# Ten of sixteen weight sums of a decoder block moved from ahead of and inside the recurrence to behind it

## The chip, the cores and the metric

One core of a Trainium2 chip runs the whole program. The metric is the device time of one execution in microseconds (us). The engines are named as in the profile: PE (TensorE), DVE (VectorE), ACT (ScalarE), POOL (GpSimd) and SP (SyncE, which here only issues transfers).

## The reference

One layer of a decoder trunk in fp32, over 2048 tokens of width 1024: a gated linear attention mixer, a 4-head attention into 256 memory tokens beside it, an output projection, and a squared-ReLU MLP of width 4096.

```
h = rms_norm(x, norm_mix)
y_mix, xq = gla_branch(h, ...)              # projections, then a chunked recurrence
y_mem = memory_cross_attention(xq, rms_norm(mem, norm_mem), w_kv)
x = x + concatenate([y_mix, y_mem]) @ w_out
x = x + sq_relu_mlp(rms_norm(x, norm_mlp), w_up, w_down)
return rms_norm(x, final_norm)
```

## The kernel before, in words

The 2048 rows are worked through in 4 blocks of 512. Block 0 is written out by itself, blocks 1 to 3 run in a loop. A block reads all weights again, in "chunks" of 1 MB: SP loads a chunk into one of two halves of `raw`, ACT rounds it to `w_hi` (`split_hi`), DVE takes the rest `w_lo = raw - w_hi` (`split_lo`), and PE makes three products of each pair of operands. Chunk `i` is loaded when the parts of chunk `i - 2` have been made, and split when PE is done with chunk `i - 2`.

A block has these stages, by chunk number: queries of the memory attention (0, 1), then q, k (2 to 5; with the gate's running sum, on DVE, line 1290, and the memory attention), v and the output gate r (6 to 13), the output projection (`C_OUT` = 14 to 19), and the MLP (from `C_MLP` = 20; its chunks are counted by `s` from 0). In stage 6 to 13 the recurrence runs beside the projections: 16 half steps `hs`, each a ring of POOL (products with decays, `rung_products`), PE (`L1694`), DVE (gaps) and ACT (exponentials).

The MLP's order is 5 "up" chunks, 7 "down" chunks, 4 up, 7 down, 4 up, 7 down, 3 up, 7 down. The down product is made by a scheme with 7 products instead of 8 on sums of quarters of the activations (DVE, `u_parts`) and of the weights. The weights' sums don't depend on the block. So they are made once, in block 0, in 16 steps of 1 MB, and kept in DRAM in `w_mix`. Of each seven down chunks four are read from `w_mix` and three from `w_down`. One step `j` is: SP loads two rows of quarters of `w_down` into a slot (`mix_load`), POOL makes four subtractions of 128x512 in place (`mix_sums`, lines 652 to 659), and SP stores the slot (`mix_store`). A slot is a piece of on-chip memory that something else uses at other times. In the kernel before there are three: a piece over `y_rows` and the inner state, the upper half of `sr`, and `u_parts`. The first two are in use during the recurrence's later half, and `u_parts` in the MLP.

SP works through its own list in order. Where the transfers of the sums stand in it is a table by chunk number, written by hand (`mix_work`). A load of a slot waits until the slot's last store has landed. A store waits for POOL's sums. Everything behind them on SP, the chunk loads too, waits with them. The kernel before does steps 0 to 11 on POOL ahead of the recurrence's first product, and steps 12 to 15 behind half steps 1, 3, 7 and 9 of the recurrence in block 0.

`xres` holds the block's residual rows; it is loaded at `C_OUT + 3`. `xin` holds the next block's x; it is loaded at MLP position `s` = 4, squared by ACT and scaled by DVE later in the MLP, and transposed by PE in the last seven down chunks. Block 0's own x was in `xin` and is last read at some 50 us.

Of the kernel before, what the change touches and what calls it, by code (L numbers as in the profile page):

```python
# [96 lines left out]
C_OUT = C_R + 4  # L97
# [12 lines left out]
UPS = HIDDEN // FCOLS  # L110
GROUPS = 4
DEPTH = UPS // GROUPS
RING = DEPTH + 1
HALF = BLOCK // 2
OPERANDS = 7
# [15 lines left out]
PIECES = 2  # L131

MIX_STEPS = UPS
MIX_EARLY = 12
MIX_LATE = {1: 12, 3: 13, 7: 14, 9: 15}

STEPS = 2 * (C_OUT - C_V)

# [135 lines left out]
def build(nc, x, mem, norm_mix, norm_mem, w_kv, w_out, norm_mlp, w_up, w_down, w_in, w_gate2, b_gate,  # L274
          out_gain, final_norm, rung_masks, identity, scan_mask, w_mix, out):
    with ExitStack() as ctx:
# [3 lines left out]
        def sem(name):  # L280
            return ctx.enter_context(nc.semaphore(name))
# [75 lines left out]


        mix_slots = [over_y_and_state[:], sr[:, 4:8, :], u_parts[:].rearrange("p (b x) t -> p b (x t)", b=4)]
        a_parts = u_parts[:, 0:4:3, :]  # L360
        b_parts = u_parts[:, 1:3, :]

# [65 lines left out]
        sums_ready = Signal(sem("sums_ready"), 0, UPS)  # L428
        u_hi_ready = Signal(sem("u_hi_ready"), 0, 2 * UPS)
        u_ready = Signal(sem("u_ready"), 2, 2 * UPS)  # L430
        mix_loaded = [sem(f"mix_loaded{s}") for s in range(3)]
        mix_made = sem("mix_made")
        mix_step = sem("mix_step")
        mix_stored = [sem(f"mix_stored{s}") for s in range(3)]
        out_ready = Signal(sem("out_ready"), 0, TILES)
        dve_step = sem("dve_step")

# [76 lines left out]
        def last_piece(i):  # L514

            return PIECES * i + PIECES - 1

        def mix_slot(j):

            return j % 3 if j < MIX_EARLY else 1 + j % 2  # L520

        def mix_uses(j):

# [2 lines left out]
        def mlp_source(s):  # L526

            if MLP[s][0] == "up":
                return wup[:, :, FCOLS * MLP[s][1]:FCOLS * (MLP[s][1] + 1)], KD
            g, operand = MLP[s][1], PRODUCTS[MLP[s][2]][2]  # L530
            if operand >= T1:
                return w_mix[:, g, operand - T1, :, :], DEPTH
            row, col = {B11: (0, 0), B21: (1, 0), B22: (1, 1)}[operand]
            return wdown[:, 2 * DEPTH * g + row:2 * DEPTH * (g + 1):2, 512 * col:512 * (col + 1)], DEPTH

# [19 lines left out]
        @block.sync  # L555
        def _(sp):
            def load(n, i, source, kblocks):

                sp.wait_ge(*hi_split.at(n, last_piece(i - 2)))
                sp.wait_ge(*lo_split.at(n, last_piece(i - 2)))  # L560
                sp.dma_start(as_kblocks(raw, i % 2, kblocks), source).then_inc(raw_loaded[i % 2].sem, 16)

            def mix_load(j):

                slot = mix_slot(j)
                if mix_uses(j):
                    sp.wait_ge(mix_stored[slot], 16 * mix_uses(j))
                to = mix_slots[slot].rearrange("p (k d) c -> p k (d c)", k=2)
                sp.dma_start(to, wdown[:, 2 * j:2 * j + 2, :]).then_inc(mix_loaded[slot], 16)

            def mix_store(j):

                slot = mix_slot(j)
                sp.wait_ge(mix_made, j + 1)
                sp.dma_start(w_mix[:, j // DEPTH, :, j % DEPTH, :], mix_slots[slot]).then_inc(mix_stored[slot], 16)

            mix_work = {1: [(mix_store, 0), (mix_load, 2)], 2: [(mix_store, 1), (mix_load, 3)],
                        3: [(mix_store, 2), (mix_load, 4), (mix_store, 3), (mix_load, 5)],
                        4: [(mix_store, 4), (mix_load, 6), (mix_store, 5), (mix_load, 7)],
                        5: [(mix_store, 6), (mix_load, 8), (mix_store, 7), (mix_load, 9)],  # L580
                        6: [(mix_store, 8), (mix_load, 10), (mix_store, 9), (mix_load, 11)],
                        7: [(mix_store, 10), (mix_store, 11)], 8: [(mix_load, 12), (mix_load, 13)],
                        10: [(mix_store, 12)], 11: [(mix_load, 14), (mix_store, 13)], 12: [(mix_load, 15)],
                        13: [(mix_store, 14)], 15: [(mix_store, 15)]}

            def load_block(n, x_row, x_next, first):
                for i in range(1, C_MLP):
                    load(n, i, chunk_source(i), KD if i < C_V or C_R <= i < C_OUT else KG)
                    if first:
                        for work, j in mix_work.get(i, ()):  # L590
                            work(j)
                    if i == C_OUT + 3:

                        sp.wait_ge(*read(n, ("oT", TILES - 1, 1)))
                        sp.dma_start(xres[:, :, :], x_tiles[:, bass.ds(x_row, TILES), :])\
                            .then_inc(xres_loaded.sem, 16)
                for s in range(len(MLP)):
                    if s == DEPTH:

                        sp.wait_ge(*weights_used.at(n, last_piece(C_MLP - 1)))  # L600
                        sp.dma_start(xin[:, :, :], x_tiles[:, bass.ds(x_next, TILES), :])\
                            .then_inc(xin_loaded.sem, 16)
                        for slot in range(3):
                            sp.wait_ge(mix_stored[slot], 16 * sum(mix_slot(j) == slot for j in range(MIX_STEPS)))
                    load(n, C_MLP + s, *mlp_source(s))
                load(n, CHUNKS, chunk_source(0), KD)

            sp.dma_start(xres[:, 0:MT, :], mem_tiles).then_inc(mem_loaded, 16)
            for i in range(KV_CHUNKS):
                if i >= 2:  # L610
                    sp.wait_ge(*hi_split.early(last_piece(i - 2)))
                    sp.wait_ge(*lo_split.early(last_piece(i - 2)))
                sp.dma_start(as_kblocks(raw, i % 2, KD), wkv[:, :, FCOLS * i:FCOLS * (i + 1)])\
                    .then_inc(raw_loaded[i % 2].sem, 16)
                if i == 1:
                    sp.dma_start(xin[:, :, :], x_tiles[:, 0:TILES, :]).then_inc(xin_loaded.sem, 16)
                    for tile, source in [(wg_raw, win[:, :, COL_G:COL_G + RANK]), (scan_raw, scan_mask),
                                         (masks_raw, rung_masks), (gain_o[:], out_gain), (gate_bias[:], b_gate),
                                         (gain_mlp[:], norm_mlp),
                                         (gain_fin[:], final_norm.rearrange("(a d) -> a d", a=1).broadcast_to([P, D]))]:  # L620
                        sp.dma_start(tile, source).then_inc(consts_loaded, 16)
            load(0, 0, chunk_source(0), KD)
            mix_load(0)
            mix_load(1)
            load_block(0, 0, TILES, True)
            with sp.Fori(1, BLOCKS) as n:
                load_block(n, sp.snap(n * TILES), sp.snap(((n + 1) % BLOCKS) * TILES), False)
# [3 lines left out]
        def _(pool):  # L631
# [29 lines left out]

            for j in range(MIX_EARLY):
                mix_sums(j)

            def rung_products(n, c, rung):


# [26 lines left out]
            def pool_block(n, first):  # L694
                for f in range(2):

                    pool.wait_ge(*read(n, ("k", 2 + f)))
                def o_rsqrt(c):
                    pool.wait_ge(*o_ms_ready.at(n, c))
                    nc.gpsimd.tensor_tensor(o_rstd[:, c, :], o_ms[:, c, :], minus_half[:], ALU.pow)\  # L700
                        .then_inc(o_rstd_ready.sem, 1)

                def y_low(c, p):
                    pool.wait_ge(*y_hi_ready.at(n, p * TILES + c))
                    hi = at_chunk(h_hi[:, 4 * p:4 * p + 4, :].bitcast(F32), c)
                    nc.gpsimd.tensor_tensor(at_chunk(h_lo[:, 4 * p:4 * p + 4, :], c), heads_of(y_row(c)), hi,  # L706
                                            ALU.subtract).then_inc(mix_ready.sem, 1)

                for hs in range(STEPS):
                    c = hs // 4  # L710
                    rung_products(n, c, hs % 4)
                    if hs % 4 == 0 and c:
                        end_products(n, c - 1)
                    if hs in (10, 12, 14):
                        o_rsqrt(hs // 2 - 5)
                    if first and hs in MIX_LATE:
                        mix_sums(MIX_LATE[hs])
                end_products(n, TILES - 1)
                o_rsqrt(TILES - 1)
                for p in range(2):  # L720
                    for c in range(TILES):
                        y_low(c, p)
                for which in range(3):
                    for t in range(TILES):
                        rsqrt(n, which, t)

            pool_block(0, True)
            with pool.Fori(1, BLOCKS) as n:
# [1271 lines left out]
```

## Time and profile before

| | |
|---|---|
| median of 3 runs | 2612.5 us (2611.78 to 2613.19) |
| the profiled execution | 2613.3 us, its span 2611.5 us |
| PE busy | 2540.9 us (97% of the span) |
| DVE, ACT, POOL busy | 59%, 46%, 17% |
| DMA | 339 MB, mean 130 GB/s |

The span runs from the first to the last instruction of the profiled execution; its own time is 1.8 us more. Idle time of an engine ahead of an instruction is shown with what ended it, as `[2.75 <-DVE u_lo L1456]`. `x2` behind a row says that it merges two instructions. SPq rows are transfers being issued; their landing is shown in another view.

### The profile page before, as it was taken

Reading aid. Unit: us, or ns where it says so; the run is one execution under the profiler, and the core shown is the slowest. Engines: PE = TensorE matmul, PEld = TensorE weight load, DVE = VectorE, ACT = ScalarE, POOL = GpSimd, SP = SyncE. Lnnn points to the kernel's source line nnn. Section 1 sums busy time; section 2 is a strip of 40 time slices with the busy share of each in tenths; the row PEclk is TensorE's granted clock in tenths of the full one; section 3 lists DMA queues with packets and bytes.
Section 4 is the critical chain, followed back from the end, with each engine's and each line's share of the span. In section 5 each row is a group of like instructions: output and inputs, shape, how many; then the busy total and the mean of one; then the engine's idle time right before and its main releaser. Section 6 shows DMA issues by size and latency. Waiting matters only on the chain.

```text
span 2611.5 us, 34630 instructions
## 1 busy us (share of the span) xinstructions
PE 2540.9 (97%) x11968; PEld 2125.4 (81%) x11968; DVE 1546.5 (59%) x2255; ACT 1205.5 (46%) x1752; POOL 445.6 (17%) x411
## 2 busy tenths in 40 slices
PE   6898999999999999999999999999999999999998
PEld 5687888888878888888878888888887888888886
DVE  5566646566746644666565663565665566465666
ACT  4433435444554434454445342545545444355444
POOL 4656400000003430000000541000000254000000
PEclk9999999999999999999999999999999999999999
DMA  8843234344422223443452213344433221343443
GB/s 295 295 164 122 65 115 167 122 161 146 165 95 65 65 100 127 148 136 122 144 178 65 81 50 119 123 149 158 145 131 129 81 65 53 124 163 124 150 155 135
DMA packets 191880, 339.41 MB, mean 130 GB/s; under 512 B 7025, under 2 KB 118769, under 8 KB 183505
## 3 DMA queue, kind: packets, MB, share of 16 engines
q1 hardware_dynamic: 188768, 328.36, 37.8%
q10 hardware_dynamic: 2928, 8.66, 0.8%
q8 instruction: 108, 1.77, 0.3%
q14 instruction: 76, 0.61, 0.1%
HBM read 311.84 MB, written 25.17 MB: 129 GB/s over the span
## 4 chain that ended last, share of the span: by engine, by line
issue 48%; PE 40%; POOL 5%; DVE 4%; ACT 1%; DMA 1%; DVEq 0%; ACTq 0%; POOLq 0%; SPq 0%
PE banks L1548 11%; PE banks L1550 11%; PE banks L1549 11%; PE banks L1694 3%; POOL queries L681 2%; PE banks L1674 1%; POOL h_lo L706 1%; POOL rstd L638 1%; PE banks L1735 1%; PE banks L1733 1%; PE banks L1718 1%; POOL keys L679 1%; DVE w_lo L1090 1%; DMA raw<-in_w_kv 1%; DVE sr L1288 1%
## 5 line engine op out<-in xcount | busy, mean ns | idle before, releaser
L1548 PE MATMUL banks<-h_hi,w_hi 128*128 128x512 f32 (+1 forms) x1760 | 678.1, 385 | 11.5 <-DVE h_lo L1109 4.7
L1550 PE MATMUL banks<-h_hi,w_lo 128*128 128x512 f32 (+1 forms) x1760 | 669.5, 380 | 0.0
L1549 PE MATMUL banks<-h_lo,w_hi 128*128 128x512 f32 (+1 forms) x1760 | 669.4, 380 | 0.0
L1090 DVE TENSOR_TENSOR w_lo<-raw,w_hi 128x2048 fp32r<-128x2048 f32 x144 | 344.9, 2395 | 296.5 <-ACT w_hi L738 296.5
L738 ACT ACTIVATE w_hi<-raw 128x2048 fp32r<-128x2048 f32 x144 | 275.5, 1913 | 271.2 <-PE banks L1548 241.8
L1548 PEld LDWEIGHTS banks<-h_hi,w_hi 128*128 128x128 f32 x1760 | 332.1, 189 | 77.5 <-issue 16.3
L1550 PEld LDWEIGHTS banks<-h_hi,w_lo 128*128 128x128 f32 x1760 | 331.8, 189 | 63.4
L1549 PEld LDWEIGHTS banks<-h_lo,w_hi 128*128 128x128 f32 x1760 | 332.1, 189 | 61.1
L1548 PE MATMUL banks<-w_hi,u_hi 128*128 128x512 f32 x896 | 351.8, 393 | 0.0
L1550 PE MATMUL banks<-w_hi,u_lo 128*128 128x512 f32 x896 | 349.1, 390 | 0.0
L1549 PE MATMUL banks<-w_lo,u_hi 128*128 128x512 f32 x896 | 348.8, 389 | 0.0
L745 ACT ACTIVATE w_hi<-raw 128x1024 fp32r<-128x1024 f32 x224 | 230.3, 1054 | 235.0 <-PE banks L1548 137.9
L1097 DVE TENSOR_TENSOR w_lo<-raw,w_hi 128x1024 fp32r<-128x1024 f32 x224 | 265.2, 1218 | 82.5 <-ACT w_hi L745 82.4
L638 POOL TENSOR_TENSOR rstd<-ms,minus_half 128x1 f32<-128x1 f32 x48 | 30.1, 631 | 1511.0 <-DVE ms L1101 1511.0
L1384 DVE TENSOR_TENSOR xres<-banks,xres 128x512 f32<-128x512 f32 x256 | 173.3, 688 | 120.0 <-PE banks L1550 119.3
L1548 PE MATMUL banks<-w_hi,h_hi 128*128 128x512 f32 (+1 forms) x544 | 215.0, 395 | 1.6 <-ACT v L813 1.2
L999 ACT ACTIVATE u_parts<-banks 128x512 f32<-128x512 f32 x128 | 76.2, 596 | 295.3 <-PE banks L1550 168.2
L1550 PE MATMUL banks<-w_hi,h_lo 128*128 128x512 f32 (+1 forms) x544 | 209.1, 384 | 0.0
L1549 PE MATMUL banks<-w_lo,h_hi 128*128 128x512 f32 (+1 forms) x544 | 209.1, 384 | 0.0
L1550 PEld LDWEIGHTS banks<-w_hi,u_lo 128*128 128x128 f32 x896 | 168.2, 188 | 35.4
L1549 PEld LDWEIGHTS banks<-w_lo,u_hi 128*128 128x128 f32 x896 | 168.3, 188 | 34.1
L1548 PEld LDWEIGHTS banks<-w_hi,u_hi 128*128 128x128 f32 x896 | 168.3, 188 | 33.9
(162 smaller groups left out, 3166.6 us busy)
## 6 DMA issues: line engine op xcount, KB each, us to landing
raw<-in_w_up SPq DMA_DIRECT2D x64, 1024.0 KB, 5.4
raw<-w_mix SPq DMA_DIRECT2D x64, 1024.0 KB, 4.7
raw<-in_gla_w_in SPq DMA_DIRECT2D x57, 1024.0 KB, 5.1
raw<-in_w_down SPq DMA_DIRECT2D x48, 1024.0 KB, 4.6
raw<-in_w_out SPq DMA_DIRECT2D x24, 1024.0 KB, 4.9
xin<-in_x SPq DMA_DIRECT2D x5, 2048.0 KB, 11.6
xres<-in_x SPq DMA_DIRECT2D x4, 2048.0 KB, 7.8
out<-xres ACTq DMA_DIRECT2D x16, 512.0 KB, 3.6
```

The lines of the kernel that those rows point to most:

```text
L638: nc.gpsimd.tensor_tensor(rstd[:, which, t:t + 1], ms[:, which, t:t + 1], minus_half[:, 0:1], ALU.pow).then_inc(rstd_ready.sem, 1)
L681: last = nc.gpsimd.tensor_tensor(kind_cols(queries, w, kind), spans(at_chunk(q, c), w, first, count), kind_cols(query_dec, w, kind), ALU.mult)
L738: nc.scalar.activation(w_hi[:, i % 2, :], raw[:, i % 2, :], ACT.Copy).then_inc(hi_split.sem, PIECES)
L745: nc.scalar.activation(w_hi[:, i % 2, at], raw[:, i % 2, at], ACT.Copy).then_inc(hi_split.sem, 1)
L999: nc.scalar.activation(part, banks[:, f, :].rearrange("p (h t) -> p h t", h=2), ACT.Relu)\
L1090: nc.vector.tensor_tensor(w_lo[:, i % 2, :], raw[:, i % 2, :], w_hi[:, i % 2, :].bitcast(F32), ALU.subtract).then_inc(lo_split.sem, PIECES)
L1097: nc.vector.tensor_tensor(w_lo[:, i % 2, at], raw[:, i % 2, at], w_hi[:, i % 2, at].bitcast(F32), ALU.subtract).then_inc(lo_split.sem, 1)
L1384: nc.vector.tensor_tensor(xres[:, t, cols], bank(name), xres[:, t, cols], ALU.add)\
L1548: after_chunk(pe.matmul(to, left[0], right[0], start=start, stop=False, skip_group_check=goes_on))
L1549: pe.matmul(to, left[0], right[1], start=False, stop=False, skip_group_check=goes_on)
L1550: return pe.matmul(to, left[1], right[0], start=False, stop=stop, skip_group_check=goes_on)
L1694: ins = pe.matmul(bank(name)[:, (h % 2) * COLS:(h % 2 + 1) * COLS], left, queries[:, h, :], start=True, stop=True)
```

## The change

Steps 0 to 5 stay ahead of the recurrence, in the same three slots. Steps 6 to 15 get two new slots, the two halves of `xin`. POOL makes sums 6 and 7 behind its last work for the mixer's output (`y_low`), and sums 8 to 15 behind the four `rsqrt` of the MLP's norm. SP loads slots for 6 and 7 behind the load of `xres` at chunk `C_OUT + 3`, and the other transfers stand in the MLP's first 14 chunks. The next x is now loaded at `s` = 15 in every block, once both new slots have been stored, which is ahead of up chunk 8 instead of up chunk 4.

```
-MIX_EARLY = 12
-MIX_LATE = {1: 12, 3: 13, 7: 14, 9: 15}
+NEXT_X = 15
+MIX_EARLY = 6
+MIX_IN_OUT = 8
...
+        mix_slots += [xin[:, 2 * s:2 * s + 2, :].rearrange("p t (b c) -> p (t b) c", b=2) for s in range(2)]
...
-            return j % 3 if j < MIX_EARLY else 1 + j % 2
+            return j % 3 if j < MIX_EARLY else 3 + j % 2
...
                 for s in range(len(MLP)):
-                    if s == DEPTH:
+                    if s == NEXT_X:
                         sp.wait_ge(*weights_used.at(n, last_piece(C_MLP - 1)))
+                        for slot in range(3, 5):
+                            sp.wait_ge(mix_stored[slot], 16 * sum(mix_slot(j) == slot for j in range(MIX_STEPS)))
                         sp.dma_start(xin[:, :, :], x_tiles[:, bass.ds(x_next, TILES), :])\
                             .then_inc(xin_loaded.sem, 16)
...
-                    if first and hs in MIX_LATE:
-                        mix_sums(MIX_LATE[hs])
                 end_products(n, TILES - 1)
                 o_rsqrt(TILES - 1)
                 for p in range(2):
                     for c in range(TILES):
                         y_low(c, p)
+                if first:
+                    for j in range(MIX_EARLY, MIX_IN_OUT):
+                        mix_sums(j)
                 for which in range(3):
                     for t in range(TILES):
                         rsqrt(n, which, t)
+                    if first and which == 0:
+                        for j in range(MIX_IN_OUT, MIX_STEPS):
+                            mix_sums(j)
```

In the loads of the MLP, SP also waits, ahead of each first down chunk, until the stores are done that its group reads.

POOL, in block 0, the first two products of the recurrence, in the kernel before: between the products of half step 1 (`keys`, `queries`) and those of half step 2 stand the four subtractions of step 12, in the slot in `sr`.

```order
L674 TENSOR_TENSOR queries<-q,near_dec 128x4x64
L679 TENSOR_TENSOR keys<-k,key_dec 128x512
L681 TENSOR_TENSOR queries<-q,query_dec 128x4x96
L681 TENSOR_TENSOR queries<-q,query_dec 128x4x64
L681 TENSOR_TENSOR queries<-q,query_dec 128x4x32
L652 TENSOR_TENSOR sr<-sr 128x512
L654 TENSOR_TENSOR sr<-sr 128x512
L656 TENSOR_TENSOR sr<-sr 128x512
L659 TENSOR_TENSOR sr<-sr 128x512
L679 TENSOR_TENSOR keys<-k,key_dec 128x512
L681 TENSOR_TENSOR queries<-q,query_dec 128x4x96
```

The same place in the changed kernel has the products alone; ahead of it stand 24 subtractions instead of 48.

POOL, in block 0, from the last of the mixer's output rows (`h_lo`) on, in the changed kernel: two sums of four subtractions in `xin`, the four `rstd` of the MLP's norm, and then the first of eight more sums. Before, the twelve `rstd` stood here by themselves.

```order
L721 TENSOR_TENSOR h_lo<-y_rows,h_hi 128x4x128 x2
L668 TENSOR_TENSOR xin<-xin 128x512
L670 TENSOR_TENSOR xin<-xin 128x512
L672 TENSOR_TENSOR xin<-xin 128x512
L675 TENSOR_TENSOR xin<-xin 128x512
L668 TENSOR_TENSOR xin<-xin 128x512
L670 TENSOR_TENSOR xin<-xin 128x512
L672 TENSOR_TENSOR xin<-xin 128x512
L675 TENSOR_TENSOR xin<-xin 128x512
L654 TENSOR_TENSOR rstd<-ms,minus_half 128x1 x4
L668 TENSOR_TENSOR xin<-xin 128x512
L670 TENSOR_TENSOR xin<-xin 128x512
```

SP, in block 0, from the load of `xres` to the second down chunk, in the kernel before: four up chunks, the next x, the fifth up chunk and the down chunks.

```order
L595 DMA xres<-in_x 128x4x1024
L561 DMA raw<-in_w_out 128x4x512 x2
L561 DMA raw<-in_w_up 128x8x256 x4
L601 DMA xin<-in_x 128x4x1024
L561 DMA raw<-in_w_up 128x8x256
L561 DMA raw<-in_w_down 128x4x512
```

The middle of the same stretch in the changed kernel, the third to the fifth up chunk and the first down chunk: each chunk load is now followed by a store of one step and the load of the step after the next, which goes into the same slot.

```order
L563 DMA raw<-in_w_up 128x8x256 x2
L577 DMA w_mix<-xin 128x4x512
L571 DMA xin<-in_w_down 128x2x1024
L563 DMA raw<-in_w_up 128x8x256
L577 DMA w_mix<-xin 128x4x512
L571 DMA xin<-in_w_down 128x2x1024
L563 DMA raw<-in_w_up 128x8x256
L577 DMA w_mix<-xin 128x4x512
L571 DMA xin<-in_w_down 128x2x1024
L563 DMA raw<-in_w_down 128x4x512
```

## Rows read from the trace of the kernel before

**Rows 1.** The page, its first part: busy time and share of the span.
```profile
PE 2540.9 (97%) x11968; PEld 2125.4 (81%) x11968; DVE 1546.5 (59%) x2255; ACT 1205.5 (46%) x1752; POOL 445.6 (17%) x411
```

**Rows 2.** ACT's timeline, block 0, q and k stage: start us, us, instruction.
```profile
91.50 0.66 ACT L806 ACTIVATE q<-banks 128x512 f32<-128x512 f32 x1
...
113.13 0.47 ACT L813 ACTIVATE v<-banks,neg_top 128x256 f32<-128x256 f32 x1 [11.52 <-DVE neg_top L1176]
...
123.44 1.94 ACT L738 ACTIVATE w_hi<-raw 128x2048 fp32r<-128x2048 f32 x1
```

**Rows 3.** ACT's timeline, block 1, the same three instructions.
```profile
746.87 0.65 ACT L806 ACTIVATE q<-banks 128x512 f32<-128x512 f32 x1
...
760.87 0.47 ACT L813 ACTIVATE v<-banks,neg_top 128x256 f32<-128x256 f32 x1 [3.90 <-DVE neg_top L1176]
...
769.01 1.94 ACT L738 ACTIVATE w_hi<-raw 128x2048 fp32r<-128x2048 f32 x1
```

**Rows 4.** SP's timeline: the load of xres in blocks 0 and 1.
```profile
326.81 0.37 SPq L595 DMA_DIRECT2D xres<-in_x  x1
...
957.12 0.39 SPq L595 DMA_DIRECT2D xres<-in_x  x1
```

**Rows 5.** DVE instructions by line: duration ns min/median/max, first and last start.
```profile
L1288 DVE SCALAR_TENSOR_TENSOR sr<-b,sr x16: 664/668/1715, 97.0 to 2018.2; 128x512 f32<-128x512 f32 x16
L1090 DVE TENSOR_TENSOR w_lo<-raw,w_hi x144: 2278/2293/3377, 57.6 to 2598.0; 128x2048 fp32r<-128x2048 f32 x144
L1174 DVE TENSOR_REDUCE top<-banks x32: 677/691/693, 112.1 to 2056.3; 128x2 f32<-128x512 f32 x32
```

**Rows 6.** POOL's timeline, block 0: parts of steps 11 and 12, then two rstd.
```profile
114.25 3.38 POOL L656 TENSOR_TENSOR over_y_and_state<-over_y_and_state 128x512 f32<-128x512 f32 x1
...
164.65 1.30 POOL L652 TENSOR_TENSOR sr<-sr 128x512 f32<-128x512 f32 x1
...
169.26 1.35 POOL L659 TENSOR_TENSOR sr<-sr 128x512 f32<-128x512 f32 x1
...
370.94 0.56 POOL L638 TENSOR_TENSOR rstd<-ms,minus_half 128x1 f32<-128x1 f32 x1 [40.41 <-DVE ms L1101]
...
378.40 0.55 POOL L638 TENSOR_TENSOR rstd<-ms,minus_half 128x1 f32<-128x1 f32 x1 [2.74 <-DVE ms L1101]
```

**Rows 7.** SP's timeline, block 0: the loads of chunk 4 and of MLP chunk 4.
```profile
77.65 0.37 SPq L561 DMA_DIRECT2D raw<-in_gla_w_in  x1
...
397.12 0.37 SPq L561 DMA_DIRECT2D raw<-in_w_up  x1
```

**Rows 8.** Transfers: issues, KB each, median us from issue to landing.
```profile
raw<-in_w_up SPq DMA_DIRECT2D x64, 1024.0 KB, 5.4
...
u_parts<-in_w_down SPq DMA_DIRECT2D x6, 1024.0 KB, 7.3
...
w_mix<-u_parts SPq DMA_DIRECT2D x6, 1024.0 KB, 8.7
```

**Rows 9.** PE's waits from 340 to 400 us: total, times, longest.
```profile
PE banks L1548 <- DVE h_lo L1399: 0.7, 1, 0.7
```

**Rows 10.** DVE's and ACT's timeline in block 0's MLP.
```profile
387.48 2.29 DVE L1090 TENSOR_TENSOR w_lo<-raw,w_hi 128x2048 fp32r<-128x2048 f32 x1 [0.83 <-ACT w_hi L738]
...
390.41 0.60 ACT L999 ACTIVATE u_parts<-banks 128x512 f32<-128x512 f32 x1 [3.03 <-PE banks L1550]
...
403.48 1.91 ACT L738 ACTIVATE w_hi<-raw 128x2048 fp32r<-128x2048 f32 x1
...
409.82 0.60 ACT L999 ACTIVATE u_parts<-banks 128x512 f32<-128x512 f32 x1 [2.75 <-DVE u_lo L1456]
...
413.19 0.60 ACT L999 ACTIVATE u_parts<-banks 128x512 f32<-128x512 f32 x1 [2.11 <-PE banks L1550]
...
414.36 1.91 ACT L738 ACTIVATE w_hi<-raw 128x2048 fp32r<-128x2048 f32 x1
...
450.53 2.03 ACT L745 ACTIVATE w_hi<-raw 128x1024 fp32r<-128x1024 f32 x2 [3.41 <-DMA raw<-w_mix]
```

More of the change, by code:

```diff
@@ L430, in build @@
         u_ready = Signal(sem("u_ready"), 2, 2 * UPS)
-        mix_loaded = [sem(f"mix_loaded{s}") for s in range(3)]
+        mix_loaded = [sem(f"mix_loaded{s}") for s in range(5)]
         mix_made = sem("mix_made")
         mix_step = sem("mix_step")
-        mix_stored = [sem(f"mix_stored{s}") for s in range(3)]
+        mix_stored = [sem(f"mix_stored{s}") for s in range(5)]
         out_ready = Signal(sem("out_ready"), 0, TILES)
@@ L575, in mix_store @@
                 sp.dma_start(w_mix[:, j // DEPTH, :, j % DEPTH, :], mix_slots[slot]).then_inc(mix_stored[slot], 16)
[L577 to L584, printed above, removed]
+            mix_work = {1: [(mix_load, 2)], 2: [(mix_store, 0), (mix_load, 3)], 3: [(mix_store, 1), (mix_load, 4)],
+                        4: [(mix_store, 2), (mix_load, 5)], 6: [(mix_store, 3)], 7: [(mix_store, 4)],
+                        8: [(mix_store, 5)], C_OUT + 3: [(mix_load, 6), (mix_load, 7)],
+                        C_OUT + 5: [(mix_store, 6), (mix_load, 8)], C_MLP: [(mix_store, 7), (mix_load, 9)],
+                        C_MLP + 2: [(mix_store, 8), (mix_load, 10)], C_MLP + 3: [(mix_store, 9), (mix_load, 11)],
+                        C_MLP + 4: [(mix_store, 10), (mix_load, 12)], C_MLP + 5: [(mix_store, 11), (mix_load, 13)],
+                        C_MLP + 6: [(mix_store, 12)], C_MLP + 7: [(mix_store, 13)], C_MLP + 8: [(mix_load, 14)],
+                        C_MLP + 9: [(mix_load, 15)], C_MLP + 12: [(mix_store, 14)], C_MLP + 13: [(mix_store, 15)]}
             def load_block(n, x_row, x_next, first):
@@ L588, in load_block @@
                     load(n, i, chunk_source(i), KD if i < C_V or C_R <= i < C_OUT else KG)
-                    if first:
-                        for work, j in mix_work.get(i, ()):
-                            work(j)
                     if i == C_OUT + 3:
@@ L596, in load_block @@
                             .then_inc(xres_loaded.sem, 16)
+                    if first:
+                        for work, j in mix_work.get(i, ()):
+                            work(j)
                 for s in range(len(MLP)):
-                    if s == DEPTH:
+                    if s == NEXT_X:
                         sp.wait_ge(*weights_used.at(n, last_piece(C_MLP - 1)))
+                        for slot in range(3, 5):
+                            sp.wait_ge(mix_stored[slot], 16 * sum(mix_slot(j) == slot for j in range(MIX_STEPS)))
                         sp.dma_start(xin[:, :, :], x_tiles[:, bass.ds(x_next, TILES), :])\
                             .then_inc(xin_loaded.sem, 16)
+                    if MLP[s] == ("down", 0, 0):
                         for slot in range(3):
                             sp.wait_ge(mix_stored[slot], 16 * sum(mix_slot(j) == slot for j in range(MIX_STEPS)))
+                    if s and MLP[s][0] == "down" and MLP[s - 1][0] == "up" and MLP[s][1] < GROUPS - 1:
+                        for slot in range(3, 5):
+                            made = sum(mix_slot(j) == slot for j in range(DEPTH * (MLP[s][1] + 1)))
+                            if made:
+                                sp.wait_ge(mix_stored[slot], 16 * made)
                     load(n, C_MLP + s, *mlp_source(s))
+                    if first:
+                        for work, j in mix_work.get(C_MLP + s, ()):
+                            work(j)
                 load(n, CHUNKS, chunk_source(0), KD)
@@ L722, in pool_block @@
                         y_low(c, p)
+                if first:
+                    for j in range(MIX_EARLY, MIX_IN_OUT):
+                        mix_sums(j)
                 for which in range(3):
```

## The prediction

> **What bounds the kernel now.** I read the page first: PE is busy 97% of the span [rows 1]. So only time in which PE is idle, or waits in a ring with other engines, can be won. The sums exist in block 0 alone, and block 1 does the same work without them. The next views are therefore the timelines of blocks 0 and 1, the same instruction in both, and the distance between them. Where the distance shrinks, block 0 has lost time that block 1 did not lose.
>
> - The copy of q starts at 91.50 in block 0 and at 746.87 in block 1: 655.37 apart. The split of the weights at the end of the first two score tiles starts at 123.44 and 769.01: 645.57 apart [rows 2, 3]. Block 0 loses 9.8 us between them. The reader sees where: ACT waits 11.52 us for DVE's `neg_top`, 3.90 us in block 1.
> - The load of xres is issued at 326.81 and 957.12: 630.31 apart [rows 4]. Block 0 loses another 645.57 - 630.31 = 15.3 us, all of it between 123 and 327 us, where the recurrence is.
>
> The first loss is DVE's. The gate's running sum is four pairs of an instruction `sr<-b,sr` and a scan. The first takes up to 1715 ns in block 0, against a median of 668 ns: 1.05 us more [rows 5]. If the scans are held as long, eight instructions make 8.4 us, and POOL is making sums 9 to 11 beside them. The second loss is POOL's own: step 12 takes from 164.65 to 170.61, 6.0 us [rows 6], in a ring whose next product stands behind it. Four such steps are 24 us of POOL, of which 15.3 us, or 3.8 us a step, reached the end.
>
> **What is removed.** Sums 6 to 11 leave the q and k stage and sums 12 to 15 leave the recurrence. If nothing else changed, block 0 would run both stretches as block 1 does: -9.8 - 15.3 = **-25.1 us**.
>
> **What remains ahead of the recurrence.** The six early steps are spread thinner. Step 5 is the last: its slot is stored behind the load of chunk 4, at some 78 us [rows 7]. A store lands in 8.7 us and a slot's load in 7.3 us [rows 8]: the load is issued at 87 and lands at 94 us. The sum then takes 5 to 6 us, until 99. DVE's chain begins at 97.0 [rows 5]. So at most two of its instructions are held by 1.05 us each: 0 to 2.1 us. I take +1.0, the middle, since which comes first depends on a microsecond.
>
> **What is added, the sums' time on POOL.** POOL is empty from 331 us on but for `rstd` (370.94 to 378.95, an idle stretch of 40.41 us before it) [rows 6]. Sums 6 and 7 fit in that stretch: their slots are loaded at 327 us behind the 2 MB of xres, land by 337 and 340, and the sums are done by some 349. Nothing there waits for POOL before 370.94. PE's waits from 340 to 400 us are 0.7 us in all [rows 9], so there is no idle time on PE to win, and each delay has to be judged by its slack.
>
> **Sums 8 and 9** run from 378.95 to some 391. DVE works there on the norm and then on the second MLP chunk's `w_lo`, 387.48 to 389.77. PE finishes the first chunk's bank at about 390.4 [rows 10]: 0.6 us of slack. One POOL instruction in the way costs such a `w_lo` up to 1.08 us (3377 - 2293 ns) [rows 5]: 0.5 us on PE. With a second hold in the norm it could be 2. I take +0.5, range 0 to 2.
>
> **Sums 10 to 13** fall into the up chunks, 10.88 us each (403.48 to 414.36) [rows 10]. What PE waits for next is the bank that ACT empties once DVE has written `u_lo`: ACT starts at 409.82 and is done at 410.42, PE is done with the other bank at about 413.2 [rows 10]. The slack is 2.8 us. A sum is four POOL instructions, so it holds DVE up by at most 4 x 1.05 = 4.2 us, and DVE idles in each chunk, so that nothing adds up. The high end is 1.4 us a sum, 5.6 us. But DVE is at work in about 6 of 11 us, so that two holds are likelier than four, and two fit. I take 0, range 0 to 5.6.
>
> **Sums 14 and 15** fall into the down chunks. There a chunk's split starts when its load lands (ACT's start at 450.53, after 3.41 us of waiting for the transfer) [rows 10], and two slot loads now go between those chunk loads. A load beside others lands in 7.3 instead of 5.4 us [rows 8], 1.9 us later, and DVE is held on top of it, 1.05 us. PE is gapless there too by what the page says of the whole, so some slack is there, but no row gives it. I take +0.5, range 0 to 3.
>
> **The transfers.** SP issues ten loads and ten stores in its list of chunk loads and is blocked while it waits for a store to land. From a store to the next store of the same slot it takes 8.7 (store) + 7.3 (load) + 6.0 (sum) = 22 us [rows 6, 8], and two up chunks are 21.8 us. That holds the pace, just. The chunk loads get 3 to 4 us later than the 397.12 of before [rows 7]. A chunk loaded then is split at 414.36 [rows 10], 17.2 us later, and needs 5.4 to 7.3 us to land [rows 8]. Less the 3 to 4 us that is some 7 us to spare, or 10 in all. I take 0. The next x moves by eleven chunks, but its first reader, ACT's square, stands behind the second down chunk of the next group, more than 20 us later at these paces, and 2 MB are two transfers of 5.4 us. Blocks 1 to 3 do nothing else new: 0.
>
> **The rule on the shared port.** The instruction `sr<-b,sr`, held by 1.05 us, has two inputs in on-chip memory, and the reduction from a PSUM bank, which ran at 112.1 us beside sum 11, never took over 693 ns [rows 5]. The Trainium skill, "SBUF — State Buffer", section "Who interferes with whom", states it as a rule: a VectorE instruction with two SBUF inputs and a GpSimd one that reads SBUF exclude each other, the one that comes later blocks until the first is done, and one with a PSUM input is free. By that rule the adds into xres in the down chunks are never held, and `w_lo`, `u_parts` and `u_lo` all can be. The trace agrees. The rule speaks against the change in one point: the lock works both ways, so that DVE's long `w_lo` stretches the sums, and by it the steps could fall behind the chunks. That is rival B.
>
> **The sum.** -25.1 + 1.0 + 0.5 + 0 + 0.5 = **-23.1 us**. The profiled execution took 2613.3 us, 0.8 us over the median, so I set it against both: 2613.3 - 23.1 = 2590.2, and from the median 2612.5 - 23.1 = **2589.4 us**.
>
> **Rivals.**
> - **A: DVE is held where it matters.** All the high ends at once are 2.1 + 2 + 5.6 + 3 = 12.7 us: 2612.5 - 25.1 + 12.7 = 2600. For it: sums 10 to 13 follow the landing of their loads, which follows DVE's `w_lo`, so the overlap may be the same in each chunk. Against it: the 2.8 us.
> - **B: SP's list falls behind.** A POOL instruction took 3.38 us beside `w_lo`, against 1.3 [rows 6]: 2.1 us more. Two of them in a sum and 2 us more for each transfer give 22 + 4.2 + 4 = 30 us for two chunks, 8.2 late, and three pairs 25 us. Less the 10 us to spare this puts PE 15 us behind: 2589.4 + 15 = 2604. It decides from 3 us late per pair on. Against it: the transfers would all have to be slow together.
> - **C, slower: a sum costs as much here as in the recurrence.** If each of the ten costs the 3.8 us that a late step cost, they cost 38 us, and the time is 2612.5 - 25.1 + 38 = **2625**. The place would be DVE's queue in the up and down chunks, and it decides from 2.5 us a sum. For it: PE is gapless here, so that any delay beyond the slack shows in full. Against it: in the recurrence the sum stood in POOL's own part of the ring, and here POOL has no part in one.
> - **D: nothing to be measured.** The 25 us come back as about as much loss, 2607 to 2618, by a mixture of A and B.
>
> **Chances.** Forecast (2586.5 to 2594) 0.62, A (2594 to 2600) 0.19, B and what lies between it and D (2600 to 2607) 0.08, C 0.07, D 0.04. The range reaches from 1 us under the full gain (2587.4) to the end of A: 2586.5 to 2600. A measurement of this kernel tells 0.2%, 5 us, from no change: faster 0.88, same 0.04, slower 0.08.
>
> **What would show it.** In the changed profile: ACT's wait for `neg_top` near 113 us falls from 11.5 to 4 to 6 us; xres is loaded 23 to 25 us earlier, at 302 to 304; at most one of the four `sr<-b,sr` of block 0 is over 1 us; POOL's sums stand between 313 and 440; PE's waits in the MLP of block 0 stay under 2 us; the distance from the load of xres to the first load of block 1's chunks is as before within 2 us. I would be wrong if PE's chunk pace in the first up chunks were over 10.9 us (A or C, with DVE as the releaser), or if ACT's splits there waited for transfers (B). The weakest steps are the zero for sums 10 to 13 and the zero for SP.

## The result, and the profile after

The changed kernel takes 2597.7 us in the median of 4 runs (2593.1 to 2598.5), against 2612.1 us for the kernel before: a ratio of 0.9939, 95% interval 0.9927 to 0.9952. The quotient of the two medians is 0.9945, inside that interval. The kernel is faster, by 14.4 us or 0.6%. That lies inside the range of 2586.5 to 2600, and 8.3 us above the 2589.4 of the forecast. The profiled execution took 2597.05 us, 16.25 less than the one before.

Two distances say where the time went. This is SP's timeline of the changed kernel, the load of `xres` in blocks 0 and 3, by the summary of its line (duration ns, first and last start us):

```profile
L595 SPq DMA_DIRECT2D xres<-in_x x4: 367/382/393, 302.6 to 2201.2; - x4
```

Before, block 0's stood at 326.8 [rows 4] and block 3's at 2217.4. So 24.3 us were won ahead of block 0's load of `xres`. From it to block 3's it was 1890.6 us, three times 630.2, and it is 1898.6 now: 8.0 us were lost behind it. 24.3 - 8.0 = 16.3 us is the difference of the two profiled executions.

Not all of what was won is waiting that went away. PE does the same work, 742 instructions, between 158 and 326.8 us as in block 1 between 803.6 and 957.1 us. These are the two stretches in the kernel before (length, PE's busy time and instructions; at the end the granted clock, the DMA share and GB/s):

```profile
803.60:957.10 153.50, 151.02 (x742) 129.27 (x742) 98.68 (x200) 67.69 (x129) 72.48 (x69) 1.00 0.20 62
158.00:326.80 168.80, 156.82 (x742) 132.99 (x741) 109.01 (x200) 67.29 (x128) 98.53 (x85) 0.97 0.29 94
```

Block 0's stretch is 15.3 us longer. For 5.8 us of that PE was busy, with the same instructions at a mean granted clock of 0.97 instead of 1.00, and for 9.5 us it waited. In slices of 10 us the clock is down, to 0.83 to 0.93, from 170 to 190, from 200 to 210 and from 250 to 260, each time where PE has just waited for over 2 us. In the changed kernel it is 1.00 in each slice from 70 to 330 us.

What answers to [rows 2] is ACT's timeline of the changed kernel in the q and k stage of block 0:

```profile
92.19 0.65 ACT L825 ACTIVATE q<-banks 128x512 f32<-128x512 f32 x1
...
106.45 0.47 ACT L832 ACTIVATE v<-banks,neg_top 128x256 f32<-128x256 f32 x1 [4.16 <-DVE neg_top L1195]
...
114.59 1.95 ACT L757 ACTIVATE w_hi<-raw 128x2048 fp32r<-128x2048 f32 x1
```

The wait is 4.16 us instead of 11.52, close to block 1's 3.90 [rows 3]. The stretch from the first to the last row is 22.4 us, where it was 31.9. DVE there, which answers to the first of [rows 5]:

```profile
97.65 0.95 DVE L1307 SCALAR_TENSOR_TENSOR sr<-b,sr 128x512 f32<-128x512 f32 x1 [4.57 <-ACT sr L896]
98.64 1.22 DVE L1309 TENSOR_TENSOR_SCAN b<-scanm,sr 128x512 f32<-128x512 uint8 x1
99.78 0.67 DVE L1307 SCALAR_TENSOR_TENSOR sr<-b,sr 128x512 f32<-128x512 f32 x1
```

One instruction is held up by POOL (I call that a hold), by the last sum, for 0.3 us, and no other.

The loss is in the MLP. PE's waits in block 0 of the changed kernel, to 660 us (total, times, longest), where [rows 9] had the single wait of 0.7 us from 340 to 400:

```profile
PE banks L1567 <- ACT u_parts L1018: 4.4, 3, 1.5
...
PE banks L1567 <- DVE w_lo L1109: 1.5, 1, 1.5
...
PE banks L1567 <- DVE h_lo L1418: 0.7, 1, 0.7
PE banks L1567 <- DVE w_lo L1116: 0.7, 1, 0.7
```

The three waits for ACT stand in the up chunks. PE's queue of weight loads shows more of each: idle for 5.9 us in four pieces between 366 and 425 us (before, 0.3 in one piece).

```profile
PEld banks L1567 <- issue: 5.9, 4, 1.9
```

Why ACT is late is in DVE's timeline of the changed kernel, one up chunk:

```profile
368.59 0.43 DVE L1461 TENSOR_TENSOR u_parts<-u_parts 128x256 f32<-128x256 f32 x1 [2.41 <-ACT u_parts L1021]
369.05 0.42 DVE L1462 TENSOR_TENSOR u_parts<-u_parts 128x256 f32<-128x256 f32 x1
369.40 1.52 DVE L1463 TENSOR_TENSOR u_parts<-u_parts 128x256 f32<-128x256 f32 x1
370.95 1.39 DVE L1464 TENSOR_TENSOR u_parts<-u_parts 128x256 f32<-128x256 f32 x1
372.27 3.39 DVE L1109 TENSOR_TENSOR w_lo<-raw,w_hi 128x2048 fp32r<-128x2048 f32 x1
375.58 3.18 DVE L1475 TENSOR_TENSOR u_lo<-u_parts,u_hi 128x768 fp32r<-128x768 f32 x2
...
381.24 0.43 DVE L1461 TENSOR_TENSOR u_parts<-u_parts 128x256 f32<-128x256 f32 x1 [2.48 <-ACT u_parts L1021]
```

POOL's timeline of the changed kernel over the same stretch, which is sum 10:

```profile
369.12 1.52 POOL L668 TENSOR_TENSOR xin<-xin 128x512 f32<-128x512 f32 x1 [1.79 <-DMA xin<-in_w_down]
370.59 1.47 POOL L670 TENSOR_TENSOR xin<-xin 128x512 f32<-128x512 f32 x1
372.02 1.49 POOL L672 TENSOR_TENSOR xin<-xin 128x512 f32<-128x512 f32 x1
373.59 3.22 POOL L675 TENSOR_TENSOR xin<-xin 128x512 f32<-128x512 f32 x1
```

Sum 10 starts 0.5 us after DVE's chain has begun. Sums 11, 12 and 13 start 0.8, 0.2 and 0.2 us after theirs. From there the two engines take turns: each of POOL's four subtractions holds one DVE instruction. In the kernel before, the same instructions took 0.42, 0.42, 2.29 [rows 10] and, for the pair, 2.09 us, as these two lines of DVE's timeline show:

```profile
404.41 0.42 DVE L1444 TENSOR_TENSOR u_parts<-u_parts 128x256 f32<-128x256 f32 x1
...
407.70 2.09 DVE L1456 TENSOR_TENSOR u_lo<-u_parts,u_hi 128x768 fp32r<-128x768 f32 x2
```

So the holds are 1.10 + 0.97 + 1.10 + 1.09 = 4.3 us. ACT's first instructions of the next chunks show what it does to the pace; they answer to [rows 10]:

```profile
378.79 0.60 ACT L1018 ACTIVATE u_parts<-banks 128x512 f32<-128x512 f32 x1 [5.35 <-DVE u_lo L1475]
...
391.47 0.60 ACT L1018 ACTIVATE u_parts<-banks 128x512 f32<-128x512 f32 x1 [5.34 <-DVE u_lo L1475]
...
403.99 0.60 ACT L1018 ACTIVATE u_parts<-banks 128x512 f32<-128x512 f32 x1 [4.25 <-DVE u_lo L1475]
...
416.58 0.60 ACT L1018 ACTIVATE u_parts<-banks 128x512 f32<-128x512 f32 x1 [4.32 <-DVE u_lo L1475]
```

An up chunk takes 12.7, 12.5 and 12.6 us instead of 10.9. The second down chunk's split, which PE's end with the last up chunk released at 435.18 before, stands at 417.75, 17.4 us earlier instead of 24.3, so ACT and DVE are 6.8 us behind there.

PE itself lost less. It does the same instructions in the same order in both kernels, so that equal counts mark the same point. Up to the end of the up chunks, first the kernel before and then the changed one:

```profile
0.00:427.97 427.97, 383.13 (x1911) 325.18 (x1912) 244.17 (x375) 181.55 (x306) 184.54 (x151) 0.97 0.51 176
0.00:408.92 408.92, 377.79 (x1911) 321.11 (x1912) 235.34 (x373) 181.49 (x305) 169.93 (x141) 0.98 0.48 163
```

PE's 1911th instruction starts 19.05 us earlier, where 24.26 had been won. Counted like this, the three waits in the up chunks cost 5.2 us, the wait of 0.7 us for `w_lo`, at 427, 1.0 us, and the one of 1.5 us, at 456, 1.8 us: 8.0 us together. The second of these ends before sum 14 begins, at 430.05. It is what ACT and DVE bring along from sum 13: PE has no such wait in the two runs below without sums 10 to 13, nor in the one where they start behind `u_lo` of chunks 0 to 3.

### The profile page after: what moved, and what is told of

It reads as the page before. It is cut to its first block, busy times and chain, and to the rows that moved or that the text cites. A ratio compares the mean times of both kernels' runs of the same rounds, so it can differ in the third digit from the quotient of the medians.

```text
span 2595.3 us, 34642 instructions
## 1 busy us (share of the span) xinstructions
PE 2536.1 (98%) x11968; PEld 2121.1 (82%) x11968; DVE 1545.8 (60%) x2255; ACT 1205.5 (46%) x1752; POOL 449.6 (17%) x411
## 4 chain that ended last, share of the span: by engine, by line
issue 49%; PE 40%; DVE 4%; POOL 3%; ACT 2%; DMA 1%; DVEq 0%; POOLq 0%; ACTq 0%; SPq 0%
PE banks L1567 11%; PE banks L1569 10%; PE banks L1568 10%; PE banks L1713 3%; PE banks L1693 1%; POOL queries L696 1%; POOL h_lo L721 1%; PE banks L1752 1%; PE banks L1754 1%; PE banks L1737 1%; DVE w_lo L1109 1%; POOL rstd L654 1%; DMA raw<-in_w_kv 1%; DVE sr L1307 0%; DVE u_lo L1475 0%
## 6 DMA issues: line engine op xcount, KB each, us to landing
xin<-in_x SPq DMA_DIRECT2D x5, 2048.0 KB, 10.9
```

## The experiments

All times are medians. The kernel before took 2612.1 to 2613.0 us beside them, and "lost behind xres" is the distance from block 0's to block 3's load of `xres`, less 1890.6 us.

| kernel | us | ratio to before, 95% | lost behind xres |
|---|---|---|---|
| changed, first | 2597.7 | 0.9939 (0.9927 to 0.9952) | 8.0 |
| changed, again | 2595.5 | 0.9931 (0.9917 to 0.9945) | 8.3 |
| changed, no sums 8 to 15 | 2588.3 | 0.9908 (0.9893 to 0.9924) | 0.0 |
| changed, no sums 10 to 13 | 2591.5 | 0.9920 (0.9907 to 0.9934) | 5.2 |
| sums 10 to 13 after u_lo | 2590.3 | 0.9911 (0.9896 to 0.9926) | 2.0 |
| the same, no sums 14 and 15 | 2589.2 | 0.9910 (0.9893 to 0.9926) | 0.5 |
| sums 9 to 13 after u_lo | 2605.6 | 0.9973 (0.9962 to 0.9984) | 15.8 |
| before, no sums 12 to 15 | 2597.6 | 0.9946 (0.9933 to 0.9960) | |
| before, no sums 6 to 11 | 2602.1 | 0.9965 (0.9951 to 0.9978) | |
| before, next x at position 15 | 2613.8 | 1.0000 (0.9991 to 1.0009) | |

**Without the sums from 8 on.**

```
+                if j >= 8:
+                    slot = slot[:, :, 0:1]
```

> The changed kernel with the subtractions of steps 8 to 15 cut to one column of 512: all transfers, waits and places in the queues stay, only POOL's work in the MLP is gone, so w_mix is wrong for those steps. Block 0's MLP lost 8.0 us in the changed kernel. Theory 1 (POOL's subtractions hold VectorE up in the up chunks, and a little in the down chunks): the 8.0 us come back but for some 1 us of late transfers in the down chunks, 2597.7 - 7 = 2590.7, and PE's three waits of 1.4 to 1.5 us for ACT in the up chunks are gone. Theory 2 (the stores and loads, or SP blocked behind them, make the chunks late): nothing comes back, 2597.7, and the waits stay.

It took 2588.3 us, 9.4 less than the changed kernel's first runs and 7.1 less than its second, and nothing is lost behind `xres`. All ten loads and ten stores are still there. The store behind the load of the fifth up chunk still takes 11.1 us to land, as in the changed kernel. So the transfers alone cost nothing, and the loss needs POOL's work. Theory 1 holds, and not even the 1 us that it left to the transfers is there: it had said 2590.7.

**Without sums 10 to 13.** The same edit for `10 <= j < 14`.

> The same with only the subtractions of steps 10 to 13 cut to one column, those that run beside the up chunks 1 to 4; w_mix is wrong for these. Theory 1: the 6.8 us that the up chunks lost come back, 2597.7 - 6.8 = 2590.9, and what remains over the first run is what sums 8, 9, 14 and 15 cost by holding VectorE, under 1 us. Theory 2: 2597.7. A third, that sums 8 and 9 at the MLP's norm start the delay: between, some 2595.

It took 2591.5 us, but with a spread of 2588.3 to 2595.3, and the profiled run is the slowest. In it the up chunks go at the old pace, and the time is lost later. ACT's timeline, two up chunks and three down chunks:

```profile
386.70 0.60 ACT L1020 ACTIVATE u_parts<-banks 128x512 f32<-128x512 f32 x1 [2.75 <-DVE u_lo L1477]
...
397.59 0.60 ACT L1020 ACTIVATE u_parts<-banks 128x512 f32<-128x512 f32 x1 [2.75 <-DVE u_lo L1477]
...
424.59 2.01 ACT L766 ACTIVATE w_hi<-raw 128x1024 fp32r<-128x1024 f32 x2 [4.92 <-DMA raw<-in_w_down]
430.75 2.01 ACT L766 ACTIVATE w_hi<-raw 128x1024 fp32r<-128x1024 f32 x2 [4.14 <-DMA raw<-w_mix]
435.84 2.01 ACT L766 ACTIVATE w_hi<-raw 128x1024 fp32r<-128x1024 f32 x2 [3.08 <-DMA raw<-in_w_down]
```

The chunks are 10.9 us apart, so sums 10 to 13 are what slows them. Then the splits wait for transfers, and DVE's `w_lo` are held on top of it by sums 14 and 15, while PE waits 0.9 us at 434 and 1.9 us at 452. The median is near the 2590.9 expected, but my expectation that under 1 us would remain was a miss in the profiled run, 5.2 us. The run without any sums from 8 on has the same transfers and the same pace and lost nothing, so the transfers alone don't make this loss either. It needs POOL's work as well, and of this only sums 14 and 15 stand where the time is lost. That a slow DVE had given the transfers time is my reading, and no run shows it by itself.

**The two halves of what was won**, from the kernel before, with `if j >= 12` and `if 6 <= j < 12`.

> The kernel before with the subtractions of steps 12 to 15 cut to one column; w_mix is wrong for these. If the distance between the blocks was read rightly, the four late sums cost 15.3 us: 2612.1 - 15.3 = 2596.8. If a part of that loss is the transfers' or the start of the recurrence in a block without a predecessor, less comes back: with half, 2604.5.

> The kernel before with the subtractions of steps 6 to 11 cut to one column; w_mix is wrong for these. By the reading of the trace, sums 9 to 11 beside the gate's running sum cost 9.8 us: 2612.1 - 9.8 = 2602.3, and the scans take 1.22 us each in block 0. If the loss there were the transfers' or the clock's: 2612.1.

They took 2597.6 and 2602.1 us: 15.2 and 10.7 us less than the 2612.8 beside them. The distances between the blocks had given 15.3 and 9.8. In the first of them the granted clock from 160 to 300 us is 1.00, against 0.96 in the kernel before, and from 158 us to its load of `xres` at 311.6 PE was busy for 151.1 us with 744 instructions. So the lower clock there came with the sums. DVE's scans in the second, which had gone up to 2.21 us in the kernel before (duration ns min/median/max):

```profile
L1292 DVE TENSOR_TENSOR_SCAN b<-scanm,sr x16: 1224/1224/1226, 98.3 to 2008.1; 128x512 f32<-128x512 uint8 x16
```

**The next x by itself**, in the kernel before, from position 4 to 15.

> The kernel before with the next x loaded at MLP position 15 instead of 4, and nothing else. By the prediction this costs nothing in any block: 2612.5 within 1.5 us. If the 2 MB beside the chunk loads of the second group of up chunks delay these, it is slower in each of the four blocks by the same amount, 2 to 8 us.

2613.8 us beside 2613.0, a ratio of 1.0000: nothing, as expected.

**The changed kernel again.**

> The changed kernel once more, on the chip of the next three, since its four runs lay from 2593.1 to 2598.5 us: the same median within 2 us, 2597.7, under each theory, with the same spread.

2595.5 us, 2.2 less than the first time. The loss behind `xres` is the same, 8.3 us against 8.0. What differs is the stretch ahead of it: block 0's load of `xres` stands at 300.7 instead of 302.6 us. Over all the changed kernels it lies between 300.7 and 303.9, so that differences of under 3 us between single runs say nothing of the MLP. The granted clock of the first 80 us goes with it: 0.94 in this run, 0.89 in the two with 303.7 and 303.9 us, and 0.91 in the others.

**Sums in the gap.**

```
                         for j in range(MIX_IN_OUT, MIX_STEPS):
+                            if 10 <= j < 14:
+                                pool.wait_ge(*u_ready.at(n, 2 * (j - 10) + 1))
                             mix_sums(j)
```

> The changed kernel, with all sums, but POOL starts sum 10 only when VectorE has written u_lo of up chunk 0, sum 11 after that of chunk 1, and so on to sum 13. VectorE is then idle for 4.7 us and a sum takes 5.2. Theory 1 (holds in the up chunks, and where a sum falls decides): the holds fall from four or more per chunk to one or none, the up chunks go at 10.88 us, and the 6.8 us come back; but then SP's list is the one that is late when the down chunks come, as in the run without sums 10 to 13, which came out at 2591.5: so 2592. Theory 2 (transfers alone): 2598 or more, since the stores go later.

2590.3 us (2588.7 to 2592.3), 5.2 less than the changed kernel beside it, with ranges that don't overlap. It is the fastest kernel here that does all the work. POOL's timeline of this kernel in one up chunk:

```profile
387.19 1.29 POOL L668 TENSOR_TENSOR xin<-xin 128x512 f32<-128x512 f32 x1 [5.82 <-DVE u_lo L1477]
388.44 1.30 POOL L670 TENSOR_TENSOR xin<-xin 128x512 f32<-128x512 f32 x1
389.70 1.29 POOL L672 TENSOR_TENSOR xin<-xin 128x512 f32<-128x512 f32 x1
391.07 1.30 POOL L675 TENSOR_TENSOR xin<-xin 128x512 f32<-128x512 f32 x1
```

And ACT's, the first instruction of this chunk and of the next:

```profile
387.15 0.60 ACT L1020 ACTIVATE u_parts<-banks 128x512 f32<-128x512 f32 x1 [3.00 <-DVE u_lo L1477]
...
398.14 0.60 ACT L1020 ACTIVATE u_parts<-banks 128x512 f32<-128x512 f32 x1 [3.10 <-DVE u_lo L1477]
```

The sum starts when DVE is through and takes 5.2 us, none of it stretched. Only its end touches the next chain: ACT's wait is 3.0 instead of 2.75 us. The pace is 11.0 us for 12.5 and more, and PE has no wait left in the up chunks.

**One chunk later still.** The gate from sum 9 on, `9 <= j < 14`, each behind the chunk after.

> The same with each sum one chunk later: sum 9 after u_lo of chunk 0, to sum 13 after that of chunk 4. Theory 1: the second chunk's w_lo isn't held by sum 9 either, but this cost PE nothing. SP gets each sum up to 10.9 us later and is blocked for it, so that the chunk loads of the down chunks come later: if late chunk loads cost time there, this is slower than the run before it, 2596 to 2605; if only holds cost time, it is as fast, 2592.

2605.6 us, 15.3 more than the run before it and 0.6 above the expected range. DVE is held in the up chunks here too, in one of them twice by sum 11 (1.40 and 1.51 us for 0.42), but PE waits for none of it. SP's timeline of this kernel in the down chunks (issue time, duration):

```profile
413.68 0.45 SPq L563 DMA_DIRECT2D raw<-w_mix  x1
428.47 0.36 SPq L577 DMA_DIRECT2D w_mix<-xin  x1
428.93 0.45 SPq L563 DMA_DIRECT2D raw<-in_w_down  x1
```

And ACT's, the split of the chunk that this load brings:

```profile
436.27 2.00 ACT L766 ACTIVATE w_hi<-raw 128x1024 fp32r<-128x1024 f32 x2 [13.64 <-DMA raw<-in_w_down]
```

SP stands at the store of step 13 until 428.47, since POOL has made sum 13 only then (its last subtraction starts at 427.15). The next chunk's load stands behind it, ACT waits 13.64 us for that, and PE's longest wait is 9.2 us. This is rival B's mechanism, a chunk load late behind SP's list, brought about here by the later start of the sums. Of the two outcomes expected it is the slower.

**Without sums 14 and 15**, from the kernel with sums in the gap.

> The kernel with sums 10 to 13 started after u_lo, and the subtractions of steps 14 and 15, which run beside the down chunks, cut to one column; w_mix is wrong for these two. That kernel came out at 2590.3 and the one with no sums from 8 on at 2588.3. If the 2 us between them are VectorE's w_lo held in the down chunks, they come back: 2588.3 within 1 us, and PE's wait of 1.4 us for w_lo at the start of the second group of up chunks is gone. If they are the loads and stores that stand between the chunk loads there, 2590.3 and the wait stays.

2589.2 us, 1.1 less than the 2590.3 of the kernel that it is made from, which is within their spreads. The profile tells them apart better: 0.5 us lost behind `xres` instead of 2.0, and PE's wait for `w_lo` is gone. So of the 2 us the larger part is sums 14 and 15 holding `w_lo` in the down chunks. By the medians alone it stays open.

## Why the prediction came out as it did

The total came out inside the range, but one of its terms failed, and so did three of the signs. PE's waits in block 0's MLP were to stay under 2 us and came to 7.3. The distance behind the load of `xres` was to stay within 2 us and grew by 8. And I had written that I would be wrong if the up chunks took over 10.9 us with DVE as the releaser, and they took 12.5 to 12.7. That 2597.7 still lies inside is because the range reached to the end of rival A.

- **What is removed, -25.1 us: right.** The two parts measured alone are -15.2 and -10.7 us, and the changed kernel gained 24.3 us ahead of block 0's load of `xres`, for 25.1 less the 1.0 I had taken off. Reading block 0 against block 1 gave each to 1 us. The account of the second part lacks the clock: of the 15.3 us, 5.8 were PE working at a lower granted clock (0.97 for 1.00) and not waiting. The distance between the blocks held both, so the number did not suffer.
- **What remains ahead of the recurrence, +1.0: 0.3.** The slot landed at 92 us, not at 94, so only the last subtraction met the chain.
- **Sums 8 and 9, +0.5: nothing.** ACT's first instruction of the MLP came 24.26 us earlier, as `xres` did, so PE had lost nothing to them up to there, though `w_lo` took 2.97 us for 2.29.
- **Sums 10 to 13: this is the step that failed.** It said: "DVE is at work in about 6 of 11 us, so that two holds are likelier than four, and two fit. I take 0". They cost 6.2 us: 5.2 in the up chunks and the 1.0 right behind them. The slack of 2.8 and the 1.05 a hold were right: four holds of 4.3 us less 2.8 are 1.5, which is the wait that PE shows three times. What was wrong was to count holds as if sums fell at random over the chunk. Sums 10 to 13 all started within 0.8 us of DVE's chain, and each of their four subtractions met an instruction of it. I had named this under rival A and given it too little weight. Why the phase stays the same is only argued: SP issued the four slot loads 12.8, 12.1 and 12.6 us apart, each behind the landing of a store, and the chunks took 12.7, 12.5 and 12.6 us, so the two seem to have locked together. In the run without sums 10 to 13 the last three slot loads were 12.0 and 12.3 us apart and the chunks 10.9. PE's recorded waits are 4.4 of the 5.2 us, and the idle time of its weight loads, three pieces of 1.9, 1.9 and 1.8 us, is 5.6.
- **Sums 14 and 15, +0.5: 1.8 us**, within 0 to 3. It is the wait of 1.5 us for `w_lo` at 456.
- **Transfers and SP, 0: right for this kernel, by less than I thought.** I took stores to land in 8.7 us; beside a chunk and a slot's load they take 9.7 to 11.8. I had 22 us for two steps. The slot loads were issued 12.1 to 12.8 us apart, and 12.0 and 12.3 where the chunks took only 10.9: SP held the pace only as the chunks were slowed. This alone cost nothing in the run without sums 8 to 15. With sums 14 and 15 on top 5.2 us were lost in one run, and with the sums started a chunk later 15.8. So rival B is not far off.
- **The next x, 0: right**, ratio 1.0000 by itself.
- **Rivals.** A came out, in its mechanism and half-way in its time: 2597.7 lies between 2594 and 2600. C, 3.8 us for each of ten sums, did not: the eight sums from 8 to 15 cost 8 us, 1.0 each. Four holds are 4.3 us here, of which the slack takes 2.8. In the recurrence 3.8 of a step's 6.0 us reached the end, a part of it through the lower clock, while from 366 to 412 us in the changed kernel's MLP the clock stayed at 1.00.

**The rule on the shared port.** The Trainium skill, "SBUF — State Buffer", section "Who interferes with whom", says that two SBUF inputs on VectorE contend with a GpSimd instruction that reads SBUF, the later one blocking, and that a PSUM input makes free. The runs agree: `u_parts`, `w_lo` and `u_lo` were all held in the up chunks, by 0.97 to 1.14 us at a time, and POOL by them (3.22 us for 1.3). The adds into `xres` from PSUM, with sums 14 and 15 beside some of them, stayed at their duration (ns min/median/max, the changed kernel):

```profile
L1403 DVE TENSOR_TENSOR xres<-banks,xres x256: 675/691/693, 311.8 to 2586.0; 128x512 f32<-128x512 f32 x128
```

## What to carry to other kernels

When work on POOL is moved beside a busy DVE, count its holds at their worst, one for each of its instructions, and compare that sum with DVE's slack: what triggers the work can come round at the pace of DVE's own cycle, as here, and then it does not fall at random. If it doesn't fit, tie its start to the end of DVE's run of instructions, here one wait that gave 5 us. But look then at who waits for the result: a queue that works in order, as SP here, passes a late sum on to every load behind it.

## What was not expected of the hardware

A store of 1 MB landed in 4.0 us alone, and in 9.7 to 11.8 us in the up chunks, where the DMA engines' busy share was 0.81 and 271 GB/s were moved. And two kernels that do the same up to there reach the same instruction 3 us apart (300.7 and 303.9 us) from run to run, while the distances between blocks repeat to 0.3 us. The granted clock of the first 80 us was 0.94 in the first of these runs and 0.89 in the second; why it differed is not shown.
